# Four conditioning groups of a layer's adaLN, placed between projection groups instead of ahead of them

## What is computed

```python
for layer in range(DEPTH):
    mod = jax.nn.silu(c) @ p['w_ada'][layer] + p['b_ada'][layer]
    sh_m, sc_m, g_m, sh_f, sc_f, g_f = jnp.split(mod[:, None, :], 6, axis=-1)
    h = _rmsnorm(x, p['norm_mix'][layer]) * (1 + sc_m) + sh_m
    ...
    x = x + g_m * out
    h = _rmsnorm(x, p['norm_ffn'][layer]) * (1 + sc_f) + sh_f
    x = x + g_f * _moe(h, p, layer)
```

## Time and profile before

| | |
|---|---|
| three runs | 2291.35, 2299.39, 2301.34 us (median 2299.39) |
| profiled execution | 2293.7 us, its span 2291.9 us |
| mean granted clock of TensorE in it | 0.803 |
| PE busy | 1884.3 us, 82% of the span |
| DVE, ACT, POOL busy | 600.4, 302.8, 53.4 us |
| DMA | 390 MB, 170 GB/s over the span |

### The profile page before, as it was taken

One profiled execution on the slowest core, in us unless ns is written; L12 is line 12 of the kernel. 1 busy time (PEld: TensorE's weight loads), 2 busy tenths in 40 slices (PEclk: granted clock), 3 DMA queues, 4 the chain that ended last, 5 costly groups with the idle time before them and its releaser, 6 DMA issues.

```text
span 2291.9 us, 19257 instructions
## 1 busy us (share of the span) xinstructions
PE 1884.3 (82%) x7386; PEld 1152.6 (50%) x7386; DVE 600.4 (26%) x1226; ACT 302.8 (13%) x538; POOL 53.4 (2%) x68
## 2 busy tenths in 40 slices
PE   6998587858858999999289988999868499999972
PEld 3765487747543444443166655656545344444431
DVE  1311632474130000000334215576611200000004
ACT  1111101020011111111022220110000101111100
POOL 0000000000010000000100000000000100000000
PEclk8898555575878999999589985555589599999995
DMA  9821000102548878878622220220153287887842
GB/s 395 353 83 45 1 1 1 45 34 97 239 156 300 309 289 305 303 290 288 198 111 111 79 74 0 74 74 37 60 216 147 92 307 290 305 303 289 308 144 55
DMA packets 63280, 390.01 MB, mean 170 GB/s; under 512 B 7008, under 2 KB 7392, under 8 KB 25440
## 3 DMA queue, kind: packets, MB, share of 16 engines
q1 hardware_dynamic: 47088, 321.15, 37.9%
q0 software_dynamic: 11504, 50.98, 6.6%
q10 hardware_dynamic: 4608, 16.78, 1.8%
HBM read 339.89 MB, written 48.99 MB: 170 GB/s over the span
## 4 chain that ended last, share of the span: by engine, by line
PE 74%; DVE 10%; issue 6%; DMA 5%; ACT 3%; POOL 1%; SPq 0%; DVEq 0%; ACTq 0%; POOLq 0%; PEldq 0%
PE bank L941 30%; PE bank L582 19%; PE bank L654 5%; PE bank L894 2%; PE bank L889 2%; DMA pool<-w_ada_in 2%; PE bank L865 2%; PE bank L633 2%; PE bank L884 1%; PE bank L727 1%; PE bank L881 1%; PE bank L933 1%; PE bank L694 1%; PE bank L963 1%; ACT pool L1293 1%
## 5 line engine op out<-in xcount | busy, mean ns | idle before, releaser
L941 PE MATMUL bank<-pool 128*128 128x512 f32 x1536 | 685.5, 599 | 35.4 <-PE bank L941 12.6
L941 PEld LDWEIGHTS bank<-pool 128*128 128x128 f32 x1536 | 286.1, 191 | 393.4 <-issue 387.1
L582 PE MATMUL bank<-h,pool 128*128 128x320 f32 x1280 | 355.2, 439 | 5.2 <-PE bank L582 5.2
L582 PEld LDWEIGHTS bank<-h,pool 128*128 128x128 f32 x1280 | 245.0, 193 | 114.0 <-issue 17.4
L1932 DVE COPY pool<-bank 128x512 f32<-128x512 f32 x32 | 22.1, 692 | 506.3 <-PE bank L963 506.3
L654 PE MATMUL bank<-pool 64*64 64x64 f32 (+2 forms) x920 | 118.8, 328 | 22.1 <-DVE pool L1579 16.8
L654 PEld LDWEIGHTS bank<-pool 64*64 64x64 f32 (+2 forms) x920 | 115.6, 239 | 27.5 <-DVE pool L1579 18.2
L1938 DVE TENSOR_TENSOR pool<-bank,pool 128x512 f32<-128x512 f32 x32 | 22.1, 692 | 250.7 <-PE bank L941 250.7
L582 PE MATMUL bank<-pool 128*128 128x320 f32 x256 | 71.5, 443 | 16.0 <-DMA pool<-ssd_w_out_in 15.6
L609 PE MATMUL bank<-pool,cs 128*32 128x512 f32 x384 | 56.2, 700 | 21.8 <-DMA small<-small_in 11.5
L933 PE MATMUL bank<-const,pool 128*128 128x128 f32 x256 | 36.0, 286 | 45.9 <-DMA pool<-x_rows 35.7
(11 more groups left out here) (334 smaller groups left out, 1578.0 us busy)
## 6 DMA issues: line engine op xcount, KB each, us to landing
pool<-moe_w_gate_in SPq DMA_DIRECT2D x64, 1024.0 KB, 6.2
pool<-moe_w_up_in SPq DMA_DIRECT2D x64, 1024.0 KB, 6.5
pool<-moe_w_down_in SPq DMA_DIRECT2D x64, 1024.0 KB, 4.9
pool<-w_ada_in SPq DMA_DIRECT2D x48, 1024.0 KB, 10.5
pool<-ssd_w_in_in SPq DMA_DIRECT2D x20, 1024.0 KB, 5.5
pool<-ab_w_in_in SPq DMA_DIRECT2D x16, 1024.0 KB, 12.7
pool<-x_rows SPq DMA_DIRECT2D x32, 512.0 KB, 5.5
y_rows<-pool ACTq DMA_DIRECT2D x32, 512.0 KB, 7.9
```

Source lines behind the costliest of these rows:

```text
L582: mm = pe.matmul(b[:, 0:T], ws[kk // 4][:, kk % 4, mt * P:(mt + 1) * P], rhs[:, kk * T:(kk + 1) * T], start=(kk == 0), stop=(kk == nk - 1))
L941: mm = pe.matmul(b[:, :], lhs[:, kk * CAP:(kk + 1) * CAP], ws[kk // per][:, kk % per, col:col + BANK], start=(kk == 0), stop=(kk == nk - 1))
```

## The change

Conditioning groups 4 to 7 of layer 0 leave the place ahead of the projections. PE runs one call of one group behind each of the projection groups 3, 4, 5 and 6. SP loads the groups in that order; ScalarE copies each behind the four tiles of the projection group ahead of it; VectorE adds all four biases behind the convolution, before it waits for the weights. Layer 1 keeps its order.

```diff
-COND_NORM = ([(0, g) for g in range(4, 8)], [(1, 6), (1, 7)])
+COND_NORM = ([], [(1, 6), (1, 7)])
+COND_BETWEEN = [(0, g) for g in range(4, 8)]
+BETWEEN_AT = (3, 4, 5, 6)
...
             load_cond(COND_NORM[0])
-            load_square(a["ab_w_in"], range(8))
+            for g_ in range(8):
+                load_square(a["ab_w_in"], [g_])
+                if g_ in BETWEEN_AT:
+                    load_cond([COND_BETWEEN[BETWEEN_AT.index(g_)]])
...
-            def projections(rhs, nk, groups, bank, full):
+            def projections(rhs, nk, groups, bank, full, between=()):
...
                     slot_read(full)
+                    if _g in between:
+                        conditioning([COND_BETWEEN[between.index(_g)]])
...
-                projections(h, DK, 8, bank_for_act, act_full)
+                projections(h, DK, 8, bank_for_act, act_full, BETWEEN_AT)
...
                     act.activation(zs[:, i * T:(i + 1) * T], b[:, 0:T], ACT.Silu).then_inc(act_free, 1)
+                conditioning(COND_BETWEEN[0:1])
...
                     act.activation(hq[:, i * T:(i + 1) * T], b[:, 0:T], ACT.Copy, scale=float(P) ** -0.5).then_inc(act_free, 1)
+                conditioning(COND_BETWEEN[1:2])
...
                     act.activation(hk[:, i * T:(i + 1) * T], b[:, 0:T], ACT.Sigmoid, scale=-1.0).then_inc(act_free, 1)
+                conditioning(COND_BETWEEN[2:3])
...
                     act.activation(hv[:, i * T:(i + 1) * T], b[:, 0:T], ACT.Copy).then_inc(act_free, 1)
+                conditioning(COND_BETWEEN[3:4])
...
                 convolution(UP0, CV0, AB_CONV, W("ab_conv_w"))
+                conditioning(COND_BETWEEN)
                 dve.wait_ge(weights_used, N_AB)
```

## The result

The changed kernel takes 2302.84 us (median of 22 runs, 2298.29 to 2310.94), the kernel before 2294.5 us (22 runs beside them). The ratio is 1.0033, 95% interval 1.0023 to 1.0043: slower by 7.6 us, or by 5.3 to 9.9 us. The profiled execution took 2305.51 us, its span 2303.7 us.

The account below looks back on a forecast made before the run. Bound by loads at first, then by PE. Terms -8.0 - 1.45 + 15.1 = +5.6 us, put on a start of 2296.4 us, gave 2302 us; range 2292 to 2313 us.

Parts of the forecast that it names:

- The gain: Layer 0's token scalars wait for h alone and start at 49.33 instead of 57.35 us: 8.02 us saved.
- The price: Four one-group calls between layer 0's projections, each 3.77 us on PE's path with its ScalarE copy unhidden: 15.1 us.
- The first projection's clock: Layer 0's first projection group takes 18.98 us, as in layer 1, instead of 20.43: 1.45 us gained.
- What should cost nothing: Moved loads on SP, four ScalarE copies, four VectorE additions and POOL's queue add nothing beyond PE's own wait.
- Rival 1: PE's clock falls at each insertion between projections: +11.6 to +17.7 us, 2308 to 2314 us; chance 0.14.
- Rival 2: Copies and turns hide, so only the calls' matmuls count: -1.8 us, 2294.6 us; chance 0.06.
- Rivals 3 and 4: Rival 3: late load or VectorE at an insertion, 2308 to 2318 us, chance 0.05; rival 4: no gain, 2311.5 us, 0.03.
- The signs: Trace marks named beforehand for layer 0: start times, first group about 19 us, call gaps, no load waits, clock 1.00.

Follow-up runs that it names:

- left_out: Kernel before with layer 0's conditioning groups 4 to 7 left out, loads and all, their modulations set to 0; 2285.98 us, ratio 0.9955.
- one_call: Changed kernel with all four groups in one call behind projection group 6; 2299.02 us, ratio 1.0017 against the kernel before.
- two_moved: Against the kernel before, only groups 6 and 7 move, behind projection groups 4 and 6; 2293.87 us, ratio 0.999.
- one_moved: Against the kernel before, only group 7 moves, behind projection group 6; 2292.21 us, ratio 0.9987.
- kept_turns: Against the kernel before, group 7 multiplied behind projection group 6, group 6 multiplied ahead, both turned behind the last projection; 2288.67 us, ratio 0.9974.
- none_anywhere: Kernel before with layer 0's conditioning groups 4 to 7 left out, loads and all, their modulations set to 0.5; 3583.55 us.

## Why the prediction was right

The forecast was 2302 us by +5.6 us; measured are 2302.84 us and +7.6 us (5.3 to 9.9), within half a per cent as forecast. That 2302 lies within 1 us of the measured time is in part luck: I put the start at 2296.4 us, 1.9 us above the median of the 22 runs, and made the shift 2.0 us too small (2.7 by the medians).

- **The gain, 8.02 us: right.** The token scalars start 0.06 us after h, and left_out gives 8.1 us for it alone. The cover that it relied on, eight loads landed before the first projection, held: no wait for a load is in the profile.
- **The price, 15.1 us: right in kind, 5% too high.** It is 14.4 us, 3.60 us a call instead of 3.77; the end of the turn overlaps the next projection by 0.14 us, and the wait ahead of the matmuls is 0.30 instead of 0.33 us. That the copy of a single group hides behind nothing is shown by one_call, where the copies do hide and 1.5 us vanish.
- **The first projection's clock, 1.45 us gained: not borne out as a term.** It came out at 18.91 us, as taken from layer 1, but the profiles do not show this to be an effect of the change. In eight of them, one of each kernel, this group took 18.86 to 20.43 us, and in one_call, where PE does the same as after the change up to this group and idles for 9.82 us ahead of the token scalars too, 20.32 us (the lines below). With this term left out, the sum is 14.4 - 8.0 = +6.4 us, nearer to the measured 7.6.

```profile
47.67 8.70 PE L640 MATMUL bank<-ab_tail,h 128*64 128x8 f32 x80 [9.82 <-DVE h L1441]
...
56.38 20.32 PE bank L587 x64
```

- **What should cost nothing** did: VectorE idled 17.96 us before the first turned group, the first tile behind a copy came 5.6 us after the copy's end (132.15 to 137.75 us), SP's loads were never waited for.
- **Rival 1, the clock falls at each insertion: not seen.** The groups behind the calls take 17.34 us in the chain, in this kernel (four), in two_moved and in one_moved, and the clock stays at 1.00. The rule of the Trainium skill that stood beside it ("TensorE: Matmul & The Clock Gate", section "A second HAM failure mode: psum-queue depth-cycling") did not show here: PE idled and turned for 1.7 us between 1.92 us of matmuls and a projection, seven times in the three kernels, without a fall.
- **Rival 2, copies and turns hide: not in this change**, each call shows the 0.75 us. That they can is shown by kept_turns. The rule cited there ("Perfetto Trace Analysis", section "Optimization Strategy") did not pay in the change; it did in kept_turns (-6.0 us), where only the group that came last is moved and the turns stand where PE waits anyway.
- **Rivals 3 and 4: not seen.** No load and no addition was late, and the time until 57.35 us was indeed set by the groups.
- **The signs.** The first group (18.91 us), the clock of 1.00 and the absence of load waits came as named. Three signs were missed narrowly: the token scalars started at 48.36 us and not at 49.3 to 49.5, as h came 0.97 us earlier in this execution; from group to next projection it was 3.89 and not 4.0 to 4.2 us; the last group ended at 214.75, not at 215 to 218 us.
- **One reading was wrong.** In the earlier trace rows the DMA engines are not full in the first two slices alone: the second has an 8, and so have nine later ones. No term of the sum uses it.

What I had not worked out is that two of the four groups were free where they stood: PE had multiplied groups 4 and 5 and turned both before h was there at 49.27 us. The two turns, from the kernel before:

```profile
43.95 1.03 PE L598 MATMUL bank<-const,cond 128*128 128x9 f32 x8 [0.33 <-PE bank L609]
...
48.08 1.03 PE L598 MATMUL bank<-const,cond 128*128 128x9 f32 x8 [0.42 <-PE bank L609]
```

Moving those costs 7.2 us and brings nothing; two_moved against the changed kernel shows exactly that, 6.35 + 0.85 = 7.2 us locally.

## What to carry to other kernels

Before moving work out of a wait, ask how much of it the wait hides: here half of the moved groups were free at the old place. Of the 8.1 us by which the token scalars came after h, moving the last group alone took off 4.7 us, and moving the last two took off all. A small unit put between long ones costs its own length and its round trip to another engine; take its second half to a place where the engine waits anyway, and the trip is free. A term read from one execution's clock belongs to that execution until several profiles agree on it.

## What was not expected of the hardware

The clock rises and falls at other moments in each execution. The norm sum at 32 us, the same instructions in all eight kernels, took 6.05 to 7.43 us, and h was finished between 47.62 and 49.27 us. The SSD stage took 522.9 to 529.9 us in the seven kernels other than none_anywhere, with PE busy for 472.9 to 475.8 us of it: there the clock is a part of the difference, and waits are the rest. The Trainium skill, "TensorE: Matmul & The Clock Gate", section "What's actually happening", says that the number of slow matmuls at a start differs from run to run of one kernel; these rows fit that and show such differences at later stretches too, but they are of different kernels, as none has two profiles here. So a difference of 6 to 7 us in one stage of two single profiles does not show by itself that a change caused it. And the token scalars, 80 matmuls with 8 columns, took 8.6 to 8.7 us wherever they ran at 0.50, and 6.99 us where the first 2 us had a granted clock of 1.00.
